# Half-tile products in more parts of the first two feed forwards, modulation units moved

## What is computed

```
h = h + swiglu(rms_norm(h, f_norm[layer]), f_w_gu[layer], f_w_down[layer])   # layers 0 and 1
mod = silu(c) @ w_ada + b_ada            # 6 x 1024 values, 24 units of weights
h2 = rms_norm_2(x, norm2_w) * (1 + sc2) + sh2
x = x + g2 * ((silu(h2 @ w_gate) * (h2 @ w_up)) @ w_down)                    # the third feed forward
```

## Time and profile before

| | |
|---|---|
| median of 3 runs | 2104.94 us (2104.7 to 2105.11) |
| the profiled execution | 2104.22 us, its span 2102.3 us |
| TensorE busy | 2074.3 us, 99% of the span |
| VectorE, ScalarE, GpSimd busy | 54%, 39%, 41% |
| granted clock of TensorE | upper level in all 40 slices of the span |
| layer 0's feed forward | 186 to 546 us |
| layer 1's feed forward | 888 to 1243 us |
| third feed forward | 1753 to the end |

### The profile page before, as it was taken

How to read it: one execution, slowest core, us unless ns; L and a number is a source line. 1 busy time by engine, 2 the same in 40 slices (tenths; PEclk the granted TensorE clock), 3 DMA queues, 4 the chain that set the end, 5 groups by cost and what they waited for, 6 DMA issues and landing times.

```text
span 2102.3 us, 27305 instructions
## 1 busy us (share of the span) xinstructions
PE 2074.3 (99%) x10570; PEld 1675.8 (80%) x10570; DVE 1137.5 (54%) x1785; ACT 813.9 (39%) x1243; POOL 863.0 (41%) x644
## 2 busy tenths in 40 slices
PE   8999999999999999999999999999999999999999
PEld 6888888888888444888888878676778888989898
DVE  6445542343354797445325355576664847749393
ACT  4123221222323787322122245564454535435252
POOL 5545655555542211455556534322223240342333
PEclk9999999999999999999999999999999999999999
DMA  4224333432541000243343231211112122233232
GB/s 174 100 100 150 120 140 138 160 114 77 192 131 55 21 1 7 105 159 135 130 155 120 84 123 60 81 41 60 58 43 80 42 83 98 71 111 111 91 108 93
DMA packets 35529, 206.20 MB, mean 98 GB/s; under 512 B 4192, under 2 KB 5344, under 8 KB 16096
## 3 DMA queue, kind: packets, MB, share of 16 engines
q1 hardware_dynamic: 33408, 197.89, 26.2%
q10 hardware_dynamic: 2016, 6.88, 1.0%
HBM read 200.63 MB, written 2.10 MB: 96 GB/s over the span
## 4 chain that ended last, share of the span: by engine, by line
issue 39%; PE 32%; POOL 27%; ACT 1%; DVE 0%; DMA 0%; POOLq 0%; SPq 0%; DVEq 0%; ACTq 0%
POOL WL L523 27%; PE PS L1274 9%; PE PS L895 2%; PE PS L926 2%; PE PS L908 2%; PE PS L1340 2%; PE PS L1341 2%; PE PS L1342 2%; PE PS L634 2%; PE PS L636 2%; PE PS L635 2%; PE PS L718 1%; PE PS L720 1%; PE PS L719 1%; PE PS L825 1%
## 5 line engine op out<-in xcount | busy, mean ns | idle before, releaser
L523 POOL TENSOR_TENSOR WL<-WR,WH 128x512 fp32r<-128x512 f32 (+2 forms) x528 | 703.9, 1363 | 887.2 <-ACT WH L1409 887.2
L634 PE MATMUL PS<-Hh,WH 128*128 128x512 f32 x1152 | 451.8, 392 | 9.2 <-DVE Hl L2052 7.9
L1409 ACT ACTIVATE WH<-WR 128x2048 fp32r<-128x2048 f32 (+2 forms) x133 | 237.6, 1786 | 561.5 <-PE PS L636 521.1
L635 PE MATMUL PS<-Hl,WH 128*128 128x512 f32 x1152 | 449.4, 390 | 0.0
L636 PE MATMUL PS<-Hh,WL 128*128 128x512 f32 x1152 | 449.3, 390 | 0.0
L634 PEld LDWEIGHTS PS<-Hh,WH 128*128 128x128 f32 x1152 | 216.9, 188 | 56.3 <-issue 9.0
L635 PEld LDWEIGHTS PS<-Hl,WH 128*128 128x128 f32 x1152 | 217.0, 188 | 45.8 <-issue 1.0
L636 PEld LDWEIGHTS PS<-Hh,WL 128*128 128x128 f32 x1152 | 217.0, 188 | 45.5
L634 PE MATMUL PS<-Gh,WH 128*128 128x512 f32 x416 | 161.8, 389 | 0.0
L635 PE MATMUL PS<-Gl,WH 128*128 128x512 f32 x416 | 161.8, 389 | 0.0
L636 PE MATMUL PS<-Gh,WL 128*128 128x512 f32 x416 | 161.8, 389 | 0.0
(11 more groups left out here) (354 smaller groups left out, 3717.7 us busy)
## 6 DMA issues: line engine op xcount, KB each, us to landing
WR<-wA SPq DMA_DIRECT2D x125, 1024.0 KB, 4.8
AW<-wada SPq DMA_DIRECT2D x24, 1024.0 KB, 6.9
WR<-wB SPq DMA_DIRECT2D x16, 768.0 KB, 4.2
WR<-wC SPq DMA_DIRECT2D x16, 640.0 KB, 3.9
WR<-wD SPq DMA_DIRECT2D x16, 512.0 KB, 3.4
WR<-wE SPq DMA_DIRECT2D x8, 384.0 KB, 3.1
X<-x_in SPq DMA_DIRECT2D x8, 256.0 KB, 6.0
W1K<-w1k ACTq DMA_DIRECT2D x1, 2048.0 KB, 8.8
```

Of the source, the lines that this page charges most:

```text
L523: ins = nc.gpsimd.tensor_tensor(WL[:, s, piece], WR[:, s, piece], WH[:, s, piece].bitcast(F32), ALU.subtract)
L634: nc.tensor.matmul(PS[:, b, :], wh[:, c, cols], pe_h, start=c == 0, stop=False)
L635: nc.tensor.matmul(PS[:, b, :], wh[:, c, cols], pe_l, start=False, stop=False)
L1409: nc.scalar.activation(WH[:, s, 0:n], WR[:, s, 0:n], ACT.Copy).then_inc(hi_s, 1)
```

## The change

Layers 0 and 1 now run in three parts of 8, 8 and 6 units like the third feed forward. The first part stays plain; the second and third use seven half-tile products per unit, by the same functions, now with a layer. In these layers gate and up still need the root: VectorE multiplies by RSF in `gate_sums` and in `gated`, each chained by a wait. The token combinations are made in the first part: GpSimd adds Hh and Hl (`whole_inputs`), VectorE combines, ScalarE and VectorE split. All twelve modulation units of a layer sit in the first part and its down product. The last down product has 6 chunks per tile in place of 10. The first part's down weights use WH/WL and DNH/DNL in turn, so that the sums of the next unit have their place, but not its quarters.

```diff
 SEGMENTS = [
-    ("gu0a", "A", F1), ("dn0a", "B", 8), ("gu0b", "A", F2), ("dn0b", "C", 8),
+    ("gu0a", "A", 8), ("dn0a", "D", 8), ("gu0b", "A", 8), ("dn0b", "D", 8), ("gu0c", "A", 6), ("dn0c", "E", 8),
...
@@ SP @@
-                    segment_with_ada(name, 12 * int(name[2]), (1, 3, 5, 7, 9, 11))
+                    segment_with_ada(name, 12 * int(name[2]), {0: 1, 1: 1, 2: 3, 3: 4, 4: 5, 5: 6, 6: 7})
                 elif name in ("dn0a", "dn1a"):
-                    segment_with_ada(name, 12 * int(name[2]) + 6, (3, 6))
-                elif name in ("gu0b", "gu1b"):
-                    segment_with_ada(name, 12 * int(name[2]) + 8, (1, 3, 5, 7))
+                    segment_with_ada(name, 12 * int(name[2]), {7: 0, 8: 1, 9: 2, 10: 4, 11: 5})
...
@@ GpSimd, first part @@
+                    ins.then_inc(lo_s, 1)
+                    if u in (2, 3):
+                        whole_inputs(l, 4 * (u - 2))
...
@@ ScalarE @@
+            def feed_forward(l, eps, dst=None, gain=None, both=False):
+                norm_root(eps, RSF)
+                first_part(l)
+                for m in range(2, DC):
+                    down_high(l, "a", m)
+                sums_high(FIRST[l], W_S3, s13_s, h13_s)
+                sums_high(FIRST[l], W_S2, s4_s, h24_s)
+                quarters_high(FIRST[l])
+                seven_part(l, "b")
...
@@ in quarters_high @@
+                if l < 2 and nth(n) == 0:
+                    act.wait_ge(tile_s, SEGS[f"dn{l}a"].tile0 + DC - 1)
+                if l < 2 and nth(n) == 1:
+                    act.wait_ge(ada_acc_s, 12 * l + 12)
...
@@ VectorE, gate_sums @@
+                ins = nc.vector.tensor_tensor(SG[:, n % 2, :], SNA[:, n % 2, :], PS[:, 5 + 2 * (n % 2), :], ALU.add)
+                if layer(n) < 2:
+                    chain.mark(ins)
+                    chain.wait()
+                    ins = nc.vector.tensor_tensor(SG[:, n % 2, :], SG[:, n % 2, :], RSF[:, :], ALU.mult)
+                ins.then_inc(c1_s, 1)
...
@@ VectorE, gated @@
+                dve.wait_ge(sg_s, hidden(n) + 1)
+                if layer(n) < 2:
+                    chain.mark(nc.vector.tensor_tensor(SG[:, n % 2, :], SG[:, n % 2, :], RSF[:, :], ALU.mult))
+                    chain.wait()
+                dve.wait_ge(tile_s, seven_tiles(n))
...
@@ VectorE, down product of the first part: ada = (1, 2, 4, 5) @@
+                    if m in ada:
+                        a = 8 + ada.index(m)
+                        modulation_unit(12 * l + a, a)
+                    if first is not None and m == 5:
+                        sums_one_three(first)
+                    if late and m == 6:
+                        sums_low(first, W_S3, h13_s, l13_s)
...
@@ VectorE, first part, after each unit's gate @@
+                    modulation_unit(12 * l + u, u)
+                    if u == 3:
+                        combine_tokens(l, (T1, T3, T2, T4))
+                    if u in (5, 6):
+                        for i in ((T1, T2), (T3, T4))[u - 5]:
+                            combined_low(l, i)
...
+            def feed_forward(l, next_h=None, both=False):
+                root_known()
+                first_part(l)
+                down_part(l, "a", FIRST[l], (1, 2, 4, 5))
+                seven_part(l, "b")
+                down_part(l, "b", units_of(l, "c")[0])
+                seven_part(l, "c")
...
+                residual(f"dn{l}c", next_h=next_h, both=both, lows={DC - 1: 1} if l == 1 else {})
```

More of the change, by code:

```diff
@@ L27 @@
 FC = F // P
-F1, F2 = 12, 10
 NB = 4
@@ L447, in segment, with segment_with_ada @@
                     loop(sp, 0, seg.bodies, [], body)
-            def segment_with_ada(name, first, units):
+            def segment_with_ada(name, first, after):
                 seg = SEGS[name]
@@ L453, in segment_with_ada @@
                     load_unit(seg, u % seg.upb, u // seg.upb)
[L454 to L458, removed]
+                    for a in range(12):
+                        if after.get(a) == u:
+                            if a == 0:
+                                sp.dma_start(CROW[:, :], consts[:, C_COND:C_COND + D]).then_inc(crow_s, 16)
+                            load_ada(first + a, a % 2)
             sp.dma_start(par[:, 0:DC], par_in[:, 0:DC]).then_inc(gain_s, 16)
@@ L576, in last_down @@
                     pool.wait_ge(lo_s, u)
-                    high, low = (x[s][:, W_S2:W_S4 + 1, :].rearrange("p q m -> p (q m)") for x in (HS, LS))
+                    high, low = down_weights(l, part, u)
                     for j in range(2):
@@ new lines, in down_high @@
+            def down_high(l, part, m):
+                seg = SEGS[f"dn{l}{part}"]
+                u = seg.unit0 + m
+                s = u % 2
+                act.wait_ge(raw_s[s], 16 * (u // 2 + s))
+                if m >= 2:
+                    act.wait_ge(tile_s, seg.tile0 + m - 1)
+                elif part == "a" and l < 2:
+                    act.wait_ge(tile_s, seg.tile0 - 2 + 2 * m)
+                else:
+                    n = next(n for n in range(len(SEVEN)) if seven_unit(n) == u - 2)
+                    act.wait_ge(made_s, made(n, P3))
+                high, _ = down_weights(l, part, u)
+                nc.scalar.activation(high[:, 0:seg.size], WR[:, s, 0:seg.size], ACT.Copy).then_inc(hi_s, 1)
@@ L1681, in _ @@
             dense_squares("wo", Hh1, "f_norm1")
[L1682 removed]
+            feed_forward(1, EPS1, both=True)
             def qk_tile(r, n):
@@ new lines, in seven_part @@
+            def seven_part(l, part):
+                of_part = units_of(l, part)
+                for n in of_part:
+                    more, opening = n < of_part[-1], n == of_part[0]
+                    if not opening:
+                        up_sums(n - 1)
+                    if n == of_part[1]:
+                        sums_low(n, W_S2, h24_s, lo_s)
+                    if more:
+                        sums_one_three(n + 1)
+                    if not opening:
+                        gated(n - 1)
+                    if more:
+                        quarters_low(n + 1)
+                    if not opening:
+                        gated_low(n - 1)
+                    if more:
+                        sums_low(n + 1, W_S3, h13_s, l13_s)
+                    if more and not opening:
+                        sums_low(n + 1, W_S2, h24_s, lo_s)
+                    gate_sums(n)
+                up_sums(n)
+                gated(n)
+                gated_low(n)
```

777 lines of the change are left out of this document (387 added, 390 removed), and 1 row of the table SEGMENTS.

## The result

The changed kernel takes **2131.78 us**, median of 4 runs (2130.11 to 2132.48); the kernel before, on the same chip, 2105.03 (2104.70 to 2105.89). The ratio is 1.0125, 95% interval 1.0108 to 1.0143: slower by 26.7 us. The forecast was 2110, with a range up to 2117. The sign was right, the size was not.

The account below looks back on a forecast made before the run. TensorE, busy 99% of the span, was taken as the bound. A 23.0 us gain from shorter units was outweighed by stalls and longer ends, summing to +5.2 us: 2110 us against the median, range 2101 to 2117.

Parts of the forecast that it names:

- 28 units change their kind: Units of the second and third parts, two layers: half-tile form gains 0.82 us each if nothing waits, -23.0 us.
- steady units, 16: Later half-tile units: the root's multiplications make each last 10.68 us, 0.62 us of stall each, +9.9 us.
- openings of the parts: Start of second and third parts: an extra low part makes the third unit's product 4 late, +7.2 us.
- first to second part: Passage between these parts: quarters_high waits for the down weights' buffer and low quarters come late, +3.0 us.
- first part: Modulation and combinations hidden on VectorE, GpSimd's additions slightly late for unit 4: +1.8 us, bounds 0 and +4.
- layer 0's end: Before wq: the weight chain stays while the down tile covering it is 2.7 us shorter, +2.7 us.
- layer 1's end: Shorter down tiles leave X complete 4.8 us after TensorE's end in place of 1.2, +3.6 us.
- 15 + 10 + 6 = 31: First part on GpSimd: low parts and ten microseconds of additions end at 231, TensorE wanting unit 4 at 230.3.
- Clock: Rival: TensorE's clock falls at layer 1's end and wq, 3 us each time, 2113 to 2116; chance 0.15.
- Port: Rival: in 16 steady units the second multiplication waits for GpSimd's sum, 7 us more, 2117; chance 0.08.
- Room: Rival: VectorE keeps up in half-tile units, so 17 us of unit stalls go, 2093; chance 0.10.
- Short ends: Rival: unit stalls as forecast, but the ends and first part cost nothing, 2102 to 2106; chance 0.22.

Follow-up runs that it names:

- up_first: Changed kernel with up_sums issued ahead of the root's first multiplication in the half-tile units, same work: 2119.2 us.
- fold_root: Changed kernel with the root's second multiplication moved out of all units onto the tiles of the down products: 2133.5 us.
- short_first: Changed kernel with only the first part's eight modulation reductions a layer cut to 64 of 1024 columns: 2117.7 us, one execution.
- wq_fill_short: Changed kernel with 22 unread filling matmuls on TensorE between layer 0's last down product and wq: 2127.4 us.
- combined: Changed kernel with up_sums first, HN by ScalarE, first-part combinations spread over later units, low parts at both ends by VectorE: 2105.5 us, ratio to before 0.9999.
- all_b: combined with layer 1's two low parts later, 12 filling matmuls before wq, and the second multiplication moved onto down tiles in the second part alone: 2104.0 us.

## Why the prediction was wrong, by its own steps

| step | predicted | measured in the traces |
|---|---|---|
| 28 units change their kind | -23.0 | -23.0 (10.06 us a unit without the root) |
| steady units, 16 | +9.9 | 16 x (10.78 - 10.07) = +11.4 |
| openings of the parts | +7.2 | +7.5 |
| first to second part | +3.0 | 1.5 ahead of it, 1.8 in its first unit: +3.3 |
| first part | +1.8 | 2 x 6.8, less the 1.5 = **+12.1** |
| layer 0's end | +2.7 | 4.0 + 2.1 = **+6.1** |
| layer 1's end | +3.6 | **+6.3** |
| not foreseen | | +2.3 |
| sum | +5.2 | +26.0 |

**The half-tile units were nearly right**: 20.1 us of stalls forecast, 22.1 measured (the second part 85.82 us where the same eight take 79.12 in the third feed forward, the third 62.62 where it is 59.03, in two layers, and 1.5 us ahead of the second parts), and the mechanism was right too: the idle 0.73 us took one multiplication, the other was paid. up_first and fold_root show which: the one ahead of up_sums is paid. The forecast had both paths to gated end at the same time, 3.49 us behind gate_sums. Taking work from the one that runs through VectorE alone leaves the other, through product 4, where it is; that is why it gave nothing.

**The first part failed**, and it is 10.3 of the 20.8 us by which the spans' difference was missed. Its fifteen tiles lasted 87.44 us where 15 x 5.44 and the norm's sum are 82.05, and its down product 44.92 in place of 43.52. The step was "15 + 10 + 6 = 31 ... where TensorE wants unit 4 at 230.3". The low parts were priced rightly in it: 15 + 6 is three times the 7.0 of the earlier trace rows, and they took 7.34 + 7.45 + 6.44 = 21.2. Three things failed. First, the 10 us of additions went by 1.26 us a piece, the price of a low part's piece without a neighbour; they took 5.66 + 6.65 = 12.3 (5.49 + 5.74 = 11.2 in short_first), so the third low part ended at 233.5 and not at 231, and already unit 3 came 1.0 us late. Second, the step looked at unit 4 alone: 3.1 of the 6 us a layer are lost there and at unit 3. Third, "hidden, as are the four combinations (some 5 us)" put a term at nothing: they held VectorE for 7.0 us (238.91 to 245.83), so unit 4's silu and, behind it on ScalarE, the high part of the seventh unit (number 6) came late. In wq_fill_short, where the clock stayed up, the rest are waits of 1.1 us at that unit and of 0.9 and 0.7 in the down product; in the changed kernel 1.6 us of it are slow matmuls. VectorE had the time for the reductions, as the step said; what it didn't have was GpSimd's. short_first takes 11.2 us out of this stretch, passage included, and 12.4 out of the whole. The bounds of 0 and +4 for this term left the 12.1 outside.

**Layer 0's end** was forecast as a chain with 2.7 us less cover. The chain got longer as well: the load landed 0.7 us behind the point from which it was counted (549.19 for tile 7's end at 548.5), the low part took 5.8 us beside VectorE and not 5.0, and the clock fell to its lower level behind the 4.4 us wait, 2.1 us more.

**Layer 1's end** was sized at an X 4.8 us behind TensorE; it came at 6.4. GpSimd's low part ended 7.2 us behind tile 7's end and not 6.6. The step then had VectorE's low part start at once, but VectorE was held for 4.64 us in an addition and had one more to do, so it started 1.07 us behind GpSimd's end (1266.40, 1265.33). Behind the 7.2 us wait the granted clock was 0.67: the sums there took 3.36 us in place of 1.82, the fillers behind them 0.4 less, so the other 1.1 of the 2.7 us missed come from there.

**The rivals.** "Clock" named the right places and a price of 3 us each; wq paid 2.1, most of it in nine matmuls that came 0.20 us later each, and layer 1's end 1.1. Both falls came behind waits longer than forecast. "Port" was looked for in the steady unit, where the time did not move; one engine slowed the other in the first part (a low part of 7.34 us, 5.03 in short_first) and at layer 1's end. The Trainium skill (SBUF — State Buffer, Who interferes with whom) has VectorE and GpSimd hold the pair of ports they share as an exclusive lock. By that, layer 1's end agrees closely: a 0.69 us addition lasted until 1265.88, the GpSimd instruction beside it until 1265.33. "Room" and "Short ends" are refuted by the 22 waits and by both ends.

What stays open: 2.3 us in places of under 1 us each (0.4 at the opening of each last down product among them), and the 2.2 us by which the medians with 22 fillers are lower than the trace explains.

## What to carry to other kernels

Price a moved instruction twice: its own time on its engine, and what it does to the duration of whatever will run beside it there. Here twelve reductions a layer were hidden on VectorE and cost 12 to 14 us through GpSimd. And when a stall follows a full engine, ask whether a step stands ahead of the one somebody waits for: reordering two instructions gave 12.5 us, removing one of the multiplications gave nothing. A gain of 0.82 us a unit, with VectorE and GpSimd late at every passage, came out level at best, even after four repairs.

## What the runs showed of the hardware

- One VectorE addition of 128x512 lasted 4.64 us in place of 0.69 beside one GpSimd instruction of 128x2048; beside GpSimd instructions of 128x512 such operations took 1.76 at wq. In these two places the longer GpSimd instruction was the worse neighbour.
- TensorE's clock did not fall behind every wait of the same length. Behind 2.0 us in the first part it fell in the changed kernel (0.79 over 232 to 240 us) and stayed at 1.00 in wq_fill_short; behind 2.7 and 2.8 us at wq it stayed in one trace and fell in another. In the changed kernel's trace it fell behind the waits of 4.4 and 7.2 us.
- It also fell where nothing had been changed: in the profiled executions of combined and all_b it was 0.54 over 1456 to 1466 us, in the mixer of the second block, behind waits of 0.9 and 1.1 us; the kernel before had 1.00 there. These two executions took 2.0 and 3.7 us more than the medians of their kernels, so a single execution can mislead by as much as the last steps were meant to gain.
- A fall of the clock in a stage that waits for its weights cost nothing (132.4 against 132.5 us); at wq, where the weights then came in time, it cost 2.1 to 2.2.
